# Hybrid mixer and expert block on one core: where the final norm's tiles lie and who loads them

## What is computed

```python
aff = softmax(h @ w_router);  gate, idx = top_k(aff.T, capacity)      # 16 experts, 128 tokens each
a = xe @ w_gate;  u = xe @ w_up                                       # 1024 -> 2048 per expert
ye = (silu(a) * u) @ w_down * gate                                    # 2048 -> 1024
x = x + g2 * scatter_add(ye, idx)
return rms_norm(x, final_g)
```

## Time and profile before

| | |
|---|---|
| median of three runs | 1775.42 us (1770.96 to 1775.69) |
| the profiled execution, its own time | 1772.78 us |
| its span, first to last instruction | 1771.0 us |
| TensorE, share of the span | 94% |
| VectorE, share of the span | 76% |
| ScalarE, share of the span | 59% |
| mean DMA rate | 278 GB/s, between 365 and 399 in most slices of the expert stage |

### The profile page before, as it was taken

How to read it: one execution, slowest core, us unless ns; L and a number is a source line. 1 busy time by engine, 2 the same in 40 slices (tenths; PEclk the granted TensorE clock), 3 DMA queues, 4 the chain that set the end, 5 groups by cost and what they waited for, 6 DMA issues and landing times.

```text
span 1771.0 us, 21856 instructions
## 1 busy us (share of the span) xinstructions
PE 1659.1 (94%) x8224; PEld 1364.7 (77%) x8224; DVE 1354.6 (76%) x1315; ACT 1039.8 (59%) x960; POOL 146.1 (8%) x137
## 2 busy tenths in 40 slices
PE   6999999999989439999999999999999999999995
PEld 2699987879767328888888888888888888888884
DVE  4575543418853578989989999989999899899897
ACT  5252121345432317777777777777777777777775
POOL 3002200002100000101101101101001011011010
PEclk9999999999999759999999999999999999999998
DMA  9116521111223639999999999999999999999996
GB/s 346 60 53 191 176 73 49 48 48 48 86 95 116 241 112 365 365 389 388 370 392 385 368 393 382 371 399 368 388 390 372 384 390 367 389 385 374 393 381 239
DMA packets 204440, 492.81 MB, mean 278 GB/s; under 512 B 5716, under 2 KB 18808, under 8 KB 204392
## 3 DMA queue, kind: packets, MB, share of 16 engines
q1 hardware_dynamic: 187616, 435.30, 66.0%
q0 software_dynamic: 13248, 47.09, 8.8%
q10 hardware_dynamic: 3528, 9.75, 1.4%
HBM read 471.07 MB, written 21.05 MB: 278 GB/s over the span
## 4 chain that ended last, share of the span: by engine, by line
PE 88%; DVE 8%; ACT 2%; DMA 1%; issue 1%; ACTq 0%; DVEq 0%; POOL 0%; POOLq 0%
PE ps L1091 84%; PE ps L1510 2%; PE ps L1462 1%; DVE topi L2008 1%; DVE topv L2007 1%; DVE affT L2010 1%; DMA moda<-in_w_mod 1%; DVE hs L1864 1%; DVE ring L2091 1%; PE ps L1418 0%; PE ps L1110 0%; ACT h2T L987 0%; DVE wl L2058 0%; ACT hs L927 0%; DVE bns L1882 0%
## 5 line engine op out<-in xcount | busy, mean ns | idle before, releaser
L2058 DVE TENSOR_TENSOR wl<-ring,wh 128x2048 fp32r<-128x2048 f32 x384 | 877.5, 2290 | 106.8 <-ACT wh L1035 106.6
L1035 ACT ACTIVATE wh<-ring 128x2048 fp32r<-128x2048 f32 x384 | 737.1, 1921 | 281.5 <-PE ps L1091 281.5
L1091 PE MATMUL ps<-wh,xeh 128*128 128x512 f32 x1024 | 404.9, 395 | 1.4 <-DVE xel L2038 1.4
L1091 PE MATMUL ps<-wh,xel 128*128 128x512 f32 x1024 | 401.7, 392 | 0.0
L1091 PE MATMUL ps<-wl,xeh 128*128 128x512 f32 x1024 | 276.6, 392 | 0.0
L1091 PEld LDWEIGHTS ps<-wh,xeh 128*128 128x128 f32 x1024 | 192.8, 188 | 42.0 <-DVE xel L2038 1.8
L1091 PEld LDWEIGHTS ps<-wh,xel 128*128 128x128 f32 x1024 | 193.0, 189 | 41.5
L1091 PEld LDWEIGHTS ps<-wl,xeh 128*128 128x128 f32 x1024 | 192.5, 188 | 41.7
L1091 PE MATMUL ps<-wh,hidh 128*128 128x512 f32 x512 | 202.7, 396 | 0.0
L1091 PE MATMUL ps<-wh,hidl 128*128 128x512 f32 x512 | 200.1, 391 | 0.0
L1091 PE MATMUL ps<-wl,hidh 128*128 128x512 f32 x512 | 138.3, 392 | 0.0
(11 more groups left out here) (369 smaller groups left out, 2007.9 us busy)
## 6 DMA issues: line engine op xcount, KB each, us to landing
ring<-in_w_gate_e SPq DMA_DIRECT2D x64, 2048.0 KB, 9.3
ring<-in_w_up_e SPq DMA_DIRECT2D x64, 2048.0 KB, 9.0
ring<-in_w_down_e SPq DMA_DIRECT2D x64, 2048.0 KB, 10.7
mbw<-in_w_mod POOLq DMA_DIRECT2D x32, 512.0 KB, 5.1
hpr<-in_w_in SPq DMA_DIRECT2D x12, 1024.0 KB, 5.5
moda<-in_w_mod SPq DMA_DIRECT2D x3, 2048.0 KB, 21.1
xs<-in_x POOLq DMA_DIRECT2D x8, 512.0 KB, 8.6
wor<-in_w_out SPq DMA_DIRECT2D x2, 2048.0 KB, 7.9
```

The costliest lines, as they stand in the source:

```text
L1035: act.activation(whv[m % 4], eview(m), ACT.Copy).then_inc(hi_done, 1)
L1091: return pe.matmul(o, l, r, start=start, stop=stop)
L2058: dve.tensor_tensor(wlv[m % 4], eview(m), whv[m % 4].bitcast(F32), ALU.subtract).then_inc(lo_done, 1)
```

## The change

The final norm's tiles get places of their own: tiles 0 to 4 in 20 KB at the offset `TAIL` that no tile of the expert stage uses, tiles 5 to 7 in the first 12 KB of slot 0 of `ring`. GpSimd loads them instead of SyncE: tiles 0 to 4 directly behind the gather of `tok`, tiles 5 to 7 when VectorE has split half 17, the last that lies in slot 0. Seven tiles instead of three are scaled within the last expert, at m = 11, 13, 15, 17, 19, 21 and 23; the eighth is scaled on VectorE behind the sums into `tok`. The load of `fgrow` stands behind the first gather.

```diff
-    EARLY = 3
+    FT = 5
+    EARLY = 7
+    FIN_AT = [11 + 2 * t for t in range(EARLY)]
...
-        finv = ring[:, :, :, :].rearrange("p s k n -> p (s k n)").rearrange("p (t d) -> p t d", t=NT)
+        fin = [at(TAIL + t * 4 * KB if t < FT else RA + (t - FT) * 4 * KB, f"fin{t}", [P, D]) for t in range(NT)]
...
             pool.wait_ge(gains_in, 16)
             pool.wait_ge(idx_ready, 1)
-            pool.dma_start(fgrow[:], final_g.partition_broadcast(P)).then_inc(gains_in, 16)
...
             pool.wait_ge(idxg_ready, 1)
             gather(0)
+            pool.dma_start(fgrow[:], final_g.partition_broadcast(P)).then_inc(gains_in, 16)
...
                 in_offset=bass.IndirectOffsetOnAxis(ap=idx_u[:, NE - 1:NE], axis=0)).then_inc(xe_in, 16)
+            for t in range(NT):
+                if t == FT:
+                    pool.wait_ge(lo_done, 2 * EC * (NE - 1) + 2 * (EC - MSLOT - 1))
+                pool.dma_start(fin[t][:], stream[t * P:(t + 1) * P, :]).then_inc(fin_in[t], 16)
             pool.wait_ge(out_in, 16 * NT)
...
-            sp.wait_ge(lo_done, 2 * EC * (NE - 1) + 2 * (EC - 2))
-            sp.wait_ge(added, 16 * (NE - 1))
-            for t in range(NT):
-                sp.dma_start(finv[:, t, :], stream[t * P:(t + 1) * P, :]).then_inc(fin_in[t], 16)
             for t in range(NT):
                 sp.wait_ge(fin_ready, t + 1)
-                sp.dma_start(out[0][t * P:(t + 1) * P, :], finv[:, t, :]).then_inc(out_in, 16)
+                sp.dma_start(out[0][t * P:(t + 1) * P, :], fin[t][:]).then_inc(out_in, 16)
...
-                    if last and m >= 2 * EC - EARLY:
-                        final_root(m - 2 * EC + EARLY)
+                    if last and m in FIN_AT:
+                        final_root(FIN_AT.index(m))
...
-                    if last_one and m >= 2 * EC - EARLY:
-                        final_scale(m - 2 * EC + EARLY)
+                    if last_one and m in FIN_AT:
+                        final_scale(FIN_AT.index(m))
...
             expert(NE - 1, False, True)
-            for t in range(EARLY, NT):
-                final_scale(t)
-
-
             dve.wait_ge(added, 16 * (NE - 1))
             dve.wait_ge(mm_done, 2 * EC * NE)
...
                 dve.tensor_tensor(tok[:, n * W:(n + 1) * W], tok[:, n * W:(n + 1) * W],
                                   yw[:, n * W:(n + 1) * W], ALU.add).then_inc(tok_sum, 1)
+            for t in range(EARLY, NT):
+                final_scale(t)
             dve.wait_ge(tok_sq, 2)
```

More of the change, by code:

```diff
@@ L1040, in final_root @@
                     act.wait_ge(froot_ready, t)
-                link(act.activation(xe[:], finv[:, t, :], ACT.Square, accum_out=stat[:, 0, t:t + 1]))
+                link(act.activation(xe[:], fin[t][:], ACT.Square, accum_out=stat[:, 0, t:t + 1]))
                 act.activation(stat[:, 1, t:t + 1], stat[:, 0, t:t + 1], ACT.Sqrt, bias=epsc[:],
@@ L2090, in final_scale @@
                     dve.wait_ge(gains_in, 32)
-                dve.scalar_tensor_tensor(out=finv[:, t, :], in0=finv[:, t, :], scalar=stat[:, 2, t:t + 1],
+                dve.scalar_tensor_tensor(out=fin[t][:], in0=fin[t][:], scalar=stat[:, 2, t:t + 1],
                                          in1=fgrow[:], op0=ALU.mult, op1=ALU.mult).then_inc(fin_ready, 1)
```

## The result

| | us |
|---|---|
| kernel before, median of 6 runs beside the changed one | 1775.45 (1770.96 to 1775.69) |
| changed kernel, median of 6 runs | 1784.97 (1780.92 to 1787.91) |
| ratio, with its 95% interval | 1.0060 [1.0048, 1.0071] |
| profiled execution of the changed kernel: own time, span | 1780.92, 1779.1 |

The changed kernel is slower by more than the 0.3% that can be told from no change, and 5.7 us above the forecast, inside its range.

What follows compares the result with a forecast made beforehand. TensorE was taken to bound the kernel up to 1751.9, with 4.5 us of VectorE alone behind it. First gather -1.7, last expert +6.1 and tail +1.2 sum to +5.6 us, forecast 1779.3, range 1769.5 to 1786.5.

Steps and rivals of the forecast that it cites:

- The first gather: Start of expert 0: moving the row load behind the gather gains between 1.0 and 2.6 us, taken as 1.7.
- The first term: At the first gather: its issue comes 0.99 us earlier without the `fgrow` load ahead of it.
- The second term: At the first gather: it no longer queues behind 512 KB, so the whole gain may reach 2.6 us, taken as 1.7.
- Tile 0: Last expert, GpSimd's queue: tile 0, behind the gather of `tok`, lands between 1712.3 and 1718.2, taken as 1713.0.
- rival "tile 0 late": Last expert: tile 0 lands only at 1718.2, 5.2 us more, +10.8 in all, 1784.5; chance 0.20.
- ScalarE at m = 11: Last expert: root with table load 2.66 us plus Silu's load 1.29; Silu at 1716.95, transposes at 1718.35 instead of 1711.91.
- ScalarE from m = 12 to 19: Last expert: ScalarE needs 13.48 us per four halves against TensorE's 11.44 and becomes the bound.
- rival "tile 0 in time": Last expert: tile 0 lands by 1708.5, before ScalarE asks, leaving only tables and roots; +1.1 us in all, 1774.8; chance 0.12.
- The clock: TensorE's clock may fall during its 6.4 us wait at the first transposes; up to 2 us of slower matmuls would be hidden.
- What a table costs: ScalarE's switches between Sqrt and Silu: each table load costs 1.29 us, with no drain on top.
- The pieces of weights: Last expert: five tiles delay weight pieces by at most 6.4 us, costed at nothing because ScalarE is later still.
- The tail: Behind the last expert: tile 7's scaling and write delay the last scatter, 1.2 us longer, bounds 0.6 and 2.9.

Runs made afterwards that it cites:

- Experiments 1 and 5: 1: changed kernel, row load ahead of the first gather again, 1783.18 us, 1.0047; 5: kernel before, only the row load moved behind the first gather, 1776.6 us, 1.0007.
- the second execution: The changed kernel run and profiled again, unaltered, beside the others on the same chip: 1782.38 us, 1.0042 to the kernel before.
- experiment 11: Changed kernel with the gather of `tok` issued behind tiles 0 to 4 instead of ahead of them: 1780.91 us, 1.0035.
- Experiment 2: Changed kernel with Identity in place of Sqrt in the final norm's roots, so ScalarE keeps Silu's table: 1778.61 us, 1.0019.
- experiment 6: Changed kernel's homes and GpSimd loads alone; row load in its old place, three tiles scaled at m = 21 to 23, five behind the expert: 1778.47 us, 1.0019.
- experiments 3, 4: Changed kernel each time. 3: tiles 0 to 4 loaded earlier, from the expert input, 1779.97 us; 4: each root behind its half's Silu or high copy, 1779.76 us.
- experiment 12: Changed kernel with row load ahead of first gather, `tok` gather behind tiles 0 to 4, and roots behind Silu: 1778.36 us, 1.0021.
- experiment 8: Changed kernel rearranged: one root for five tiles, one for three, two tiles multiplied on GpSimd, row load in its old place: 1775.8 us, 1.0007.
- experiment 10: Rearranged kernel with roots of four tiles each, loads of tiles 0 to 4 spread, no multiplications on GpSimd: 1775.23 us, 1.0001 to the kernel before.

## Why the prediction was right, and where it was wrong

**The first gather: wrong, in both terms.** Predicted -1.7 us, measured +0.9 and +0.8. The first term took the issue to come 0.99 us earlier. Counted from `topf` it came 0.32 earlier (2.89 us, not 3.21): the gather now waited for its indices, `idx_e` on VectorE, which the row load had covered. The second term took 0.7 us off the landing, for bytes no longer queued ahead. The landing took 1.2 us longer: from the start of the issue to the transposes 6.48 us in place of 5.25. Experiments 1 and 5 show the same both ways round. Why the first transfer of this queue takes longer than the second isn't settled; the 0.3 us longer issue (2.29 against 1.96) is part of it.

**Tile 0: right where the prediction's own premise held.** It put the landing at 1713.0, 12.5 us after the transposes of m = 5, from an issue of the gather that takes 2.84 us. In the execution where it took 2.76, tile 0 was there 12.24 us after that mark; where it took 0.99, 9.45 after it. The prediction took one profile's duration for a property of the instruction; in the profiles of this study it was 0.98 to 3.07 us. The rival "tile 0 late", at 1718.2, didn't come about: the 1784.5 it gave is near the measured median for other reasons.

**ScalarE at m = 11: right.** Root with load, then load: 4.07 us from the start of the root to Silu, 3.95 predicted. Transposes come 17.7 us after the mark in the second execution, predicted 17.9.

**ScalarE from m = 12 to 19: right.** Predicted 13.48 us per four halves; measured 13.61 (twice) in experiment 11, with nothing else in the way. There the rival "tile 0 in time" is what happened: it had the first transposes 13.3 us after the mark, they came at 13.42, and it gave +1.6 us for the expert, the stretch grew by 1.95. Experiment 2 adds what the prediction only said in passing: VectorE is close behind, at 12.79, a little under its estimate of 13.3.

**The clock: right once, wrong once.** The slow matmuls behind the first gap were mostly hidden (TensorE's second gap is 0.55 us, where it is 1.95 in experiment 11), but in the second execution 0.9 us of them showed, and after the third gap, where the prediction had no term, 1.6 us.

**What a table costs: right.** Seven loads stand in the last expert, each 1.28 us, and ACTIVATE follows within 0.01 to 0.03 us. By an estimate with the drain of 1.38 us in the Trainium skill, ScalarE: Activation LUTs, section What ACT_TABLE_LOAD costs, Silu at m = 11 would have come near 1720; it came at 1717.29. The measurement decides: no drain shows here.

**The pieces of weights: wrong.** The prediction costed them at nothing, as ScalarE would be later. That is true in the changed kernel and hides the cost there, but it isn't true of the change's parts: experiment 6 shows 4.78 us of waiting from the loads alone, and waits for pieces (0.67, 0.62 and 2.36 us) stand in experiments 3, 4 and 12, which gave back less than their edits promised. In the kernel before, SyncE reads the same tiles only when the last piece in `ring` has been split, behind the weights.

**The tail: right in size, in part by luck**, +1.2 predicted, +1.2 measured in both executions. The path up to the landing of tile 7's write is as predicted: scaling ends 4.1 us after the result is taken out and the write lands at 6.8. But the scatter starts 0.27 us behind that, not 0.9, so it comes only 0.56 us later than before, at 7.05 in place of the predicted 7.7. The other 0.6 us stand behind the scatter's start, where the prediction had no term: from there to the end of the span it takes 8.70 to 8.78 us in all twelve profiles with the new homes, experiment 6 among them, where nothing waits for tile 7, and 8.07 and 8.11 in the two with the old ones. No run says why.

**The sum.** Predicted +5.6. Measured in the stretches that the change touches: +6.0 and +11.7, mean 8.9 (0.9 and 0.8 gather, 3.6 and 8.6 last expert, 1.2 tail, and 0.3 and 1.0 over the 15 experts between, which no edit explains). The forecast's direction held, and its mechanism in the last expert. That 6.0 is so near 5.6 is luck: the gather was 2.6 us worse than predicted and the last expert 2.5 better, as tile 0 was early in that execution. In the other the expert was 2.5 us worse, mostly with the clock, and nothing made up for the gather. By the medians the change costs 9.5 and 7.1 us.

## What to carry to other kernels

Before moving small work into a stage where the DMA engines are full, count its bytes against the stream: 2.6 MB of tiles cost the consumer of the weights up to 4.8 us of waiting, and spreading them moved the waits. In an engine that works in order, put a moved step behind the instruction that others wait for, and group the steps that share a table: with one root for four or five tiles, the squares behind Silu and the row load in its old place the change went from +0.4 to 0.6% back to nothing, though grouping wasn't tried by itself. One cost can hide another, so test a change's parts singly, and profile twice: one profile's 2.84 us or 0.99 us may be one of two values.

## What the runs showed that I had not expected

**An indirect DMA's issue on GpSimd ends 0.9 us after VectorE's running subtraction.** The gather of `tok` took 0.98 to 3.07 us to issue. In eleven profiles it was issued while a subtraction (SBUF operands) ran, and each time it ended 0.85 to 0.91 us after that subtraction did. Before, the subtraction ended at 1702.24 and the issue at 1703.11; in experiment 12 they stand at 1707.25 and 1708.13:

```profile
1705.74 2.39 POOL L636 DMA_INDIRECT tok<-stream,idx_u  x1 [0.30 <-issue]
```

```profile
1704.96 2.29 DVE L2060 TENSOR_TENSOR wl<-ring,wh 128x2048 fp32r<-128x2048 f32 x1 [0.37 <-ACT wh L1037]
```

In experiment 11 it fell into the gap of 0.37 us between two subtractions and took 1.02; in experiments 2 and 6 it was issued beside the product that reads PSUM and took 0.99 and 0.98. In the changed kernel the plain loads behind it took 0.53 to 0.61 us each, also beside a subtraction. So whether the last scatter lands before or after one subtraction starts (the gather is issued 1.1 us before the transposes of m = 5, or 0.1) puts tile 0 where it was in one profile of the changed kernel or in the other. This is read from coincidences of ends, and wasn't tried by itself.

**Beside GpSimd's multiplications VectorE's two additions took 3.64 us in place of 1.29** (experiment 8; 1.29 again in experiment 10, without them).

**A gather that is the first transfer of GpSimd's queue lands about 1 us later** than one behind a 512 KB broadcast: from the issue to TensorE's transposes 6.3 to 6.7 us in seven profiles, against 5.2 to 5.7 in the seven others.
